# Second expert layer: results stored by token number, and down weights issued one position earlier

## The reference, cut to what matters

```python
def _route(hf, w_router, router_bias):
    scores = jax.nn.sigmoid((hf @ w_router).astype(jnp.float32))
    sel = scores + router_bias.astype(jnp.float32)
    grouped = sel.reshape(-1, N_GROUPS, EXPERTS_PER_GROUP)
    group_score = lax.top_k(grouped, TOP_K)[0].sum(-1)
    best = jnp.argmax(group_score, axis=-1)
    in_group = (jnp.arange(N_EXPERTS) // EXPERTS_PER_GROUP)[None, :] == best[:, None]
    _, idx = lax.top_k(jnp.where(in_group, sel, NEG_INF), TOP_K)
    w = jnp.take_along_axis(scores, idx, axis=-1)
    w = w / jnp.sum(w, axis=-1, keepdims=True)
    return jnp.sum(jax.nn.one_hot(idx, N_EXPERTS, dtype=jnp.float32) * w[..., None], axis=1)

def _moe(h, w_router, router_bias, w_gate, w_up, w_down):
    ...
    combine = _route(hf, w_router, router_bias).astype(h.dtype)
    y = jnp.zeros_like(hf)
    for e in range(N_EXPERTS):
        a = jax.nn.silu(hf @ w_gate[e]) * (hf @ w_up[e])
        y = y + combine[:, e:e + 1] * (a @ w_down[e])
    return y.reshape(shp)

# in the second layer, and then the end of the program:
x = x + g2 * _moe(_modulate(x, norm2[l], sh2, sc2), w_router, router_bias,
                  w_e_gate[l], w_e_up[l], w_e_down[l])
return _rmsnorm(x, final_norm)
```

## Time and profile before

| what | us |
|---|---|
| median of three runs | 1684.38 |
| the profiled execution | 1684.62 |
| its span | 1682.6 |
| outside the span | 2.0 |
| PE busy | 1587.2 (94%) |
| second layer's expert stage, from the first up_gate to the last landed result rows | 1395.9 to 1657.8 |

### The profile page before, as it was taken

One profiled execution on the slowest core, in us unless ns is written; L12 is line 12 of the kernel. 1 busy time (PEld: TensorE's weight loads), 2 busy tenths in 40 slices (PEclk: granted clock), 3 DMA queues, 4 the chain that ended last, 5 costly groups with the idle time before them and its releaser, 6 DMA issues. The chain is left out here.

```text
span 1682.6 us, 16523 instructions
## 1 busy us (share of the span) xinstructions
PE 1587.2 (94%) x6162; PEld 751.8 (45%) x6162; DVE 670.0 (40%) x1608; ACT 341.5 (20%) x782; POOL 123.6 (7%) x193
## 2 busy tenths in 40 slices
PE   5999999999999999899999979999999989998994
PEld 2444456544444445644444434445644445333331
DVE  2430068866677733511100145307867144111113
ACT  1210078820000021110100023007710021000001
POOL 1000000200000010200000020000200100110101
PEclk9999999999999999899999989999999999998998
DMA  9812141115545461699999996222178758999995
GB/s 345 273 50 100 50 168 66 39 51 150 201 151 200 150 225 48 244 349 366 386 391 393 366 355 202 100 100 76 39 227 324 276 193 292 370 388 392 389 360 210
DMA packets 176128, 380.83 MB, mean 226 GB/s; under 512 B 24430, under 2 KB 28670, under 8 KB 175912
## 3 DMA queue, kind: packets, MB, share of 16 engines
q1 hardware_dynamic: 160768, 327.17, 54.9%
q0 software_dynamic: 14272, 50.20, 7.8%
q10 hardware_dynamic: 1008, 2.38, 0.4%
HBM read 362.74 MB, written 26.80 MB: 232 GB/s over the span
## 5 line engine op out<-in xcount | busy, mean ns | idle before, releaser
L1881 PE MATMUL bank<-ring_sb,HT_sb 128*128 128x512 f32 x672 | 298.4, 599 | 3.1 <-ACT HT_sb L847 2.5
L1988 PE MATMUL bank<-ring_sb,HT_sb 128*128 128x512 f32 x544 | 240.6, 595 | 0.0
L1881 PEld LDWEIGHTS bank<-ring_sb,HT_sb 128*128 128x128 f32 x672 | 126.8, 193 | 151.8 <-issue 150.1
L1988 PEld LDWEIGHTS bank<-ring_sb,HT_sb 128*128 128x128 f32 x544 | 102.3, 190 | 135.7 <-issue 135.7
L1992 PE MATMUL bank<-ring_sb,QR_sb 128*128 128x512 f32 x288 | 129.5, 592 | 0.0
L2153 PE MATMUL bank<-ring_sb,HT_sb 128*64 128x512 f32 x480 | 106.5, 596 | 2.8 <-DMA ring_sb<-w_e_up 2.8
L2171 PE MATMUL bank<-ring_sb,QR_sb 128*128 128x512 f32 x208 | 97.8, 626 | 6.5 <-DMA ring_sb<-w_e_down 6.5
L973 ACT ACTIVATE WK_sb<-bank 128x512 f32<-128x512 f32 x36 | 21.5, 597 | 348.6 <-PE bank L1988 348.6
L2134 PE MATMUL bank<-ring_sb,HT_sb 128*128 128x512 f32 x192 | 85.4, 598 | 2.7 <-ACT HT_sb L1007 2.7
L2177 PE MATMUL bank<-ring_sb,QR_sb 128*64 128x512 f32 x304 | 73.8, 630 | 12.6 <-DMA ring_sb<-w_e_down 10.6
L1992 PEld LDWEIGHTS bank<-ring_sb,QR_sb 128*128 128x128 f32 x288 | 54.8, 190 | 68.8 <-issue 68.8
(11 more groups left out here) (336 smaller groups left out, 1708.7 us busy)
## 6 DMA issues: line engine op xcount, KB each, us to landing
ring_sb<-w_e_down SPq DMA_DIRECT2D x32, 2048.0 KB, 17.2
ring_sb<-w_mod SPq DMA_DIRECT2D x24, 2048.0 KB, 9.4
ring_sb<-w_in SPq DMA_DIRECT2D x22, 2048.0 KB, 15.0
ring_sb<-w_e_gate SPq DMA_DIRECT2D x16, 2048.0 KB, 14.8
ring_sb<-w_e_up SPq DMA_DIRECT2D x16, 2048.0 KB, 18.9
ring_sb<-w_e_gate SPq DMA_DIRECT2D x22, 1024.0 KB, 16.4
ring_sb<-w_e_up SPq DMA_DIRECT2D x22, 1024.0 KB, 14.6
ring_sb<-w_branch SPq DMA_DIRECT2D x8, 1024.0 KB, 9.9
```

Source lines behind the costliest of these rows:

```text
L1881: ins = mm(bank[j % 4][:, :], HT[:, k, P * t:P * t + P], WR[slot][:, k], start=(k == 0), stop=(k == KD - 1))
L1988: ins = mm(bank[i % 2][:, :], HT[:, k, P * t:P * t + P], WR[wg][:, k], start=(k == 0), stop=(k == KD - 1))
```

## The change

Two things change, both for the second layer alone.

- SP issues down weight q - 1 behind pair q (for q from 3 to 14), not q - 2; at q = 15 only down weight 14 stands ahead of pair 15.
- A result row is stored at the row of its token: at row `token` for the token's first expert and at `256 + token` for its second. POOL does this with an indirect DMA for each position, by the index `y_of`, and empty places get an index out of bounds and are skipped. A half position is stored in half rows, with 128 indices. Afterwards the four loads of the result rows are plain DMAs of 512 KB. Rows of tokens that sit in positions 14 and 15 are not written, so the whole table of 1280 rows is filled beforehand, as 20 copies of 64 rows of x, where 128 rows were filled before. The indices need 12 more small matmuls on PE and some small DVE operations.

```diff
@@ own_stores
-    return 0 if q >= NE - 2 else 1 if full_rows(l, q) else 2
+    return 0 if q >= NE - 2 else 1 if l or full_rows(l, q) else 2
@@ SP
-                    lag = 2 if l else 1
                     if q == NE - 1:
-                        for late in range(q - lag, q):
-                            load_expert(l, late, at[late], 2)
+                        load_expert(l, q - 1, at[q - 1], 2)
                     load_pair(l, q, at[q])
-                    if 2 * lag <= q < NE - 1:
-                        load_expert(l, q - lag, at[q - lag], 2)
+                    if 2 + l <= q < NE - 1:
+                        load_expert(l, q - 1, at[q - 1], 2)
@@ POOL, fill
-                dma(y_d[l][first_row(l, NE - 2):first_row(l, NE)], t_in["x"][0, 0:CAP]).then_inc(rows_set, 16)
+                    dma(y_d[l][first_row(l, NE - 2):first_row(l, NE)], t_in["x"][0, 0:CAP]).then_inc(rows_set, 16)
+                else:
+                    some = t_in["x"][:, 0:HALF].broadcast_to([first_row(l, NE) // HALF, HALF, D])
+                    dma(y_d[l][0:first_row(l, NE)].rearrange("(c p) d -> c p d", p=HALF), some).then_inc(rows_set, 16)
@@ POOL, stores
-                    if full_rows(l, q):
+                    if l:
+                        full = full_rows(l, q)
+                        table = y_d[l][0:2 * nq * P]
+                        eng.indirect_dma_start(table if full else table.rearrange("r (h n) -> (r h) n", h=2),
+                                               bass.IndirectOffsetOnAxis(ap=y_of[full][:, q:q + 1], axis=0),
+                                               yd[q % 2] if full else yd[q % 2][:, 0:CW], None,
+                                               bounds_check=2 * nq * P * (1 if full else 2) - 1, oob_is_err=False)\
+                            .then_inc(y_out[q % 2], 16)
+                    elif full_rows(l, q):
@@ POOL, result rows
-                    gather_outputs(y_d[l][0:first_row(l, NE)])
+                    if l == 0:
+                        gather_outputs(y_d[l][0:first_row(l, NE)])
+                    else:
+                        for t in range(nq):
+                            for k in range(2):
+                                dma(ygat[t][k], y_d[l][P * (nq * k + t):P * (nq * k + t + 1)]).then_inc(ygat_in[t], 16)
@@ DVE
+                    ts(y_of[0][:, :], bank[2][:, 2 * NE:3 * NE], 2.0, lower, ALU.mult, ALU.add)
+                    ts(y_of[1][:, :], bank[2][:, NE:2 * NE], float(MISSING), None, ALU.add)
                     ts(row_of[:, :], bank[2][:, 0:NE], float(MISSING), None, ALU.add).then_inc(slot_ready, 1)
@@ PE
+                    numbers(bank[2][:, 0:NE], P, token_at[:, 1])
+                    numbers(bank[2][:, NE:2 * NE], P, second_at)
+                    numbers(bank[2][0:HALF, 2 * NE:3 * NE], HALF, second_at)
+                    numbers(bank[2][HALF:P, 2 * NE:3 * NE], HALF, second_at).then_inc(pos_mm, 1)
```

More of the change, by code:

```diff
@@ L270, in build @@
         row_of = sb("row_of", [P, NE], I32)
+        y_of = [sb(f"y_of{i}", [P, NE], I32) for i in range(2)]
         sp_idx = sb("sp_idx", [P, 1], I32)
@@ L313, in build @@
         token_at = MB[:, 608:608 + NLAT * NE].bitcast(F16).rearrange("p (k t q) -> p k t q", k=2, t=NLAT)
-        token_no = MB[:, 784:784 + NLAT]
+        token_no = MB[:, 784:784 + 2 * NLAT].rearrange("p (k t) -> p k t", k=2)
+        second_at = MB[:, 640:640 + NLAT * NE // 2].bitcast(F16).rearrange("p (t q) -> p t q", t=NLAT)
+        y_row = MB[:, 788:788 + 2 * NLAT].rearrange("p (k t) -> p k t", k=2)
+        lower = MB[:, 792:793]
         gout_half = MB[:, D:D + CW]
@@ L1545, in _ @@
                     link(tt(r_two[:, :, 0:nq], r_row.unsqueeze(1).unsqueeze(1).broadcast_to(pick), r_o12[:, :, 0:nq], ALU.mult))
-                    ts(token_no, tabh[:, H_TOK:H_TOK + nq], -float(MISSING), None, ALU.add)
+                    for k in range(2):
+                        ts(token_no[:, k], tabh[:, H_TOK:H_TOK + nq], float(nq * P * k - MISSING), None, ALU.add)
+                        ts(y_row[:, k], tabh[:, H_TOK:H_TOK + nq], float(nq * P * k), None, ALU.add)
+                    ts(lower, tabh[:, H_TOK:H_TOK + 1], float(HALF), 2.0 * MISSING, ALU.is_ge, ALU.add)
                     link(eng.tensor_reduce(where, r_two[:, :, 0:nq], AX, ALU.add))
@@ L1550, in _ @@
                     for t in range(nq):
-                        ts(token_at[:, :, t], at_place[:, :, t], token_no[:, t:t + 1], None, ALU.mult)
+                        ts(token_at[:, :, t], at_place[:, :, t], token_no[:, 0, t:t + 1], None, ALU.mult)
+                        ts(second_at[:, t], at_place[:, 1, t], token_no[:, 1, t:t + 1], None, ALU.mult)
                     wide = [P, 2, nq, P]
@@ L1577, in _ @@
                 link(tt(share, weight, held_last, ALU.mult))
-                tt(slot_g[:, :, 0:nq], slots, at, ALU.subtract)
+                if l == 0:
+                    tt(slot_g[:, :, 0:nq], slots, at, ALU.subtract)
+                else:
+                    link(tt(r_two[:, :, 0:nq, 0], slots, y_row, ALU.subtract))
+                    link(stt(r_two[:, :, 0:nq, 1], slots, float(first_row(l, NE)), r_two[:, :, 0:nq, 0], ALU.is_ge, ALU.mult))
+                    tt(slot_g[:, :, 0:nq], r_two[:, :, 0:nq, 1], y_row, ALU.add)
                 tt(weight, weight, share, ALU.subtract)
@@ L2194, in _, with numbers @@
                     eng.wait_ge(pick_ready, 5)
-                    for i in range(2 * nq):
-                        ins = mm(bank[2][:, 0:NE], in_place[:, i // nq, i % nq], token_at[:, i // nq, i % nq],
-                                 start=(i == 0), stop=(i == 2 * nq - 1))
-                    ins.then_inc(pos_mm, 1)
+                    def numbers(dst, places, of_second):
+                        for i in range(2 * nq):
+                            k, t = divmod(i, nq)
+                            ins = mm(dst, in_place[:, k, t, 0:places], of_second[:, t] if k else token_at[:, k, t],
+                                     start=(i == 0), stop=(i == 2 * nq - 1))
+                        return ins
+                    numbers(bank[2][:, 0:NE], P, token_at[:, 1])
+                    numbers(bank[2][:, NE:2 * NE], P, second_at)
+                    numbers(bank[2][0:HALF, 2 * NE:3 * NE], HALF, second_at)
+                    numbers(bank[2][HALF:P, 2 * NE:3 * NE], HALF, second_at).then_inc(pos_mm, 1)
                 transpose_rows(1)
```

2 lines of the change are left out of this document (1 added, 1 removed).

## The result

The changed kernel takes 1693.92 us (median of 9 runs, 1689.71 to 1696.02) beside 1685.76 for the kernel before (9 runs, 1683.24 to 1690.47). The ratio is 1.0043, with a 95% interval from 1.0032 to 1.0054: 7.2 us slower (the two medians alone would give 1.0048). I had predicted 1685.6 us and no difference that can be measured. In all that follows a ratio is turned into us with 1685.4, the median of the 17 runs of before that stand beside the first experiments.

The account below looks back on a forecast made before the run. The prediction took DMA bandwidth (391 GB/s), not PE, to bound the second expert stage. Terms +10.7 - 1.6 - 3.3 - 6.7 + 0.9 + 1.2 = +1.2 us on 1684.38 gave 1685.6 us; range 1682 to 1688, widened to 1677 and 1691.

Parts of the forecast that it names:

- The step that failed: Second layer's expert stage: DMA sets the end, so each change in bytes counts as time at 391 GB/s.
- Down weight 2 ahead of pair 4: Early in the stage, pair 4 now waits behind down weight 2, which waits for down(0): cost 10.7 us, bounds 0 to 10.7.
- The debt: Pair 4's 4.19 million bytes still owed at 1438 us, 10.7 us of DMA, never repaid as DMA is full to the end.
- The rival that had it shrink: Pair 4's delay does not reach the end: sum -4.2 us if halved, -9.5 if none; 1676 us, chance 0.27.
- The thin stretch: From 1439 to 1455 us DMA moved 351 GB/s with little queued; a fuller queue gains 1.6 us.
- The pause before pair 15: From 1625 to 1633 us DMA moved 229 GB/s; the new order fills this and gains 3.3 us, bounds 0 to 3.3.
- Stores: Second layer's result stores fall from 4.72 to at most 2.10 MB, as skipped places move no data: 6.7 us saved.
- skipped places save nothing: Rival: from 1438 to 1642 us scatters pay for empty places too; sum +7.9 us, 1692.3 us, chance 0.14.
- Indices: 12 more small matmuls behind up_gate(0) and two index operations ahead of `row_of`, on PE's path to down(0): cost 0.9 us.
- The end: Result loads and final norm, issued earlier, go in ahead of the last weight, which lands last: cost 1.2 us, bounds -0.2 to 1.2.
- The fill: Table fill of 5.24 MB from 1141.19 us, done before DVE reads bias tiles at 1188.71: costs 0.
- The clock: Rival: a wait over 3 us at up_gate(15) slows PE for down(15), up to 3 us, 1688.7; chance 0.12 with a late fill.

Follow-up runs that it names:

- reverse: The kernel before with the new order of down weights up to position 8 and the old one from 9 on: ratio 1.0061 to the kernel before, +10.3 us.
- hybrid: The kernel before with the old order of down weights up to position 7 and the new one from 8 on: ratio 0.9995 to the kernel before, -0.8 us.
- order_only: The kernel before with only the new order of down weights, stores, gathers and fill as before: ratio 1.0067 to the kernel before, +11.3 us.
- dense: The changed kernel, but empty places are written to table rows that nobody reads, not skipped: ratio 1.0066 to the kernel before, +11.1 us.
- guard: The changed kernel, but POOL starts result loads and final norm only once the last down weight has landed: ratio 1.0034 to the kernel before, +5.7 us.
- stride8: The changed kernel with an expert's n-th token on row 8(n mod 8) + n div 8 of its 64-row half: ratio 1.0058 to the kernel before, +9.8 us.
- spread: The changed kernel with an expert's n-th token on row 4(n mod 16) + n div 16 of its 64-row half: ratio 1.0042 to the kernel before, +7.1 us.

## Why the prediction was wrong, by its own steps

**The step that failed** is the one all terms share: bytes divided by the mean rate of the 16 engines (391 GB/s), where the end follows the engine that is furthest behind. By halves, the order had +7.0 in its terms and measured +11.3, and the stores with their indices had -5.8 and measured -4.0, so the larger part of the miss lies in the order. By terms:

- *Down weight 2 ahead of pair 4, +10.7*: right. SP's rows in after show the step, down weight 2 and pair 4 right behind it:

```profile
1439.16 0.37 SPq L550 DMA_DIRECT2D ring_sb<-w_e_down  x1
1440.32 0.38 SPq L565 DMA_DIRECT2D ring_sb<-w_e_gate  x1
```

  The debt alone, reverse against before, is 9.5 at pair 15 where debt and thin stretch gave 9.1, and it was never repaid. The rival that had it shrink is refuted.
- *The thin stretch, -1.6*: less came of it. 2.6 us later in after, to be held against the 351 GB/s of the earlier trace rows, the row below has 368, which over 16 us is 0.7 us.

```profile
1441.60:1457.60 16.00, 16.00 (x66) 6.35 (x64) 2.40 (x4) 1.19 (x2) 2.56 (x4) 1.00 1.03 368
```

- *The pause before pair 15, -3.3*: up to pair 15 the size is about right, 3.3 at the last part in hybrid and 2.3 between reverse and order_only. But the pause was also what levelled the engines, and 1.8 of it (hybrid against before) or 2.3 (order_only against reverse) were lost again between pair 15 and the last weight. Without it the parts spread over 6.0 to 7.3 us in every kernel, for 1.6 to 2.3 where there is one.
- *Stores, -6.7*: the bytes are right (POOL's queue 6.19 MB from 1437 to 1646 before, 3.55 MB from 1441 to 1646 after; predicted 2.62 less, found 2.64). The mean engine gains 6.4 (order_only to after at pair 15), the last one 4.5, because the skipped rows do not lie on all engines alike. The rival "skipped places save nothing" is refuted (dense). That its figure, +7.9, is near the measured 7.2 is luck.
- *Indices, +0.9*: nothing found. The 16 small matmuls took 0.58 us in a place where PE's path had room:

```profile
1411.89 0.58 PE L2227 MATMUL bank<-MB_sb,QR_sb 128*128 128x16 f16 x16
```

  down(0) started 33.9 us after the first `up_gate`, and 33.5 before; 0.4 at most.
- *The end, +1.2*: undersized. From pair 15's last part to the last weight's last part it is 5.9 us in before, 9.0 in after, 5.0 in guard. So the result loads cost 4.0 us in after, and 3.1 more than in before (about 0.9 there, if guard's 5.0 holds for level engines too, which no run shows). I had POOL issue them earlier, and it did so by only 0.5 us; and I had let them share with 16 even engines, where those that were behind carried their part of the loads in turn with the weight.
- *The fill, 0*: right. The additions start at 1170.39, 27 us after the fill was issued, far ahead of 1188. The rule of the Trainium skill ("DMA: Bandwidth & Descriptors", Why a DMA increments its semaphore by 16 and not by 1) for 20 copies (10 engines, an estimate of 20 us) fits this better than the 5 engines of the earlier trace rows: from 1146 to 1160 the queue moved 3.28 MB at a share of 54.7%, that is over 5 engines.

```profile
q0 software_dynamic: 104, 3.28, 54.7%
```

- *The clock*, which I had as a rival with a price of up to 3 us: it came at down(15), behind its own wait of 3.14 us, and cost 1.7; the waits of up_gate(15), which I had named, were 2.04 and 1.71. (1685.6 + 3 is 1688.6, not 1688.7.) I had also misapplied what the Trainium skill ("TensorE: Matmul & The Clock Gate", HAM oscillation — how this bites in real kernels) says of loops that compute less than they wait. PE computed about 12 us of each 16.8, so it does not say that the half positions would run cold, and most of their down products took 3.65 us. The long stretch had more but shorter waits and a higher clock (0.99 for 0.93), which gained nothing, as DMA set the pace there.

The sum in after, from the table: the last part of pair 15 +2.8 (predicted 0.0; 1.5 of it by the order, 1.3 by the stores), the end +3.1 (1.2), together +5.9 for the last landing. Of that 0.5 is slack that before had: its last weight landed at 1656.04, 0.58 us ahead of down(15), where in after it is 0.04. (The prediction took the start at 1656.62 for the landing.) Then the clock +1.7. 5.9 - 0.5 + 1.7 = 7.1, which is the 7.0 of the rows, and 7.2 was measured. Of the 6.0 us that the prediction lacked, 2.8 are the engines that were behind at pair 15, 1.9 the result loads on those engines, 1.7 the clock, less 0.5.

What stays open: which engines are late, how an indirect DMA deals its rows out to them, and why stride8's transfers were slower.

## What to carry to other kernels

A transfer that is cut over 16 engines has landed when the slowest has. In a stretch where DMA is always busy, add the saved bytes up for the mean engine, then ask how far the last one is behind, and look at the fading of the share after the stretch for it. A short pause in the queue is not all waste, since it levels the engines. A small load that comes in late beside the last large one costs more when the engines are not level. When two edits come together, time each alone: here one was worth 4 us and the other cost 11.

## What I had not expected of the hardware

- With even loads (before) the 16 parts of one transfer drift apart from 2.1 to 5.8 us within 170 us, some 0.4 us for each position. In the twelve kernels without a pause near the end the spread at pair 15 is 6.0 to 7.3 us, and never more; perhaps because SP can't issue further ahead, which no run tried.
- Rows skipped by an indirect DMA free only some engines. Six, four or two of sixteen were late, as the rows lay.
- Result loads of 2.6 MB beside the last weight cost it 4.0 us when the engines were not level (after against guard), and by an estimate from the same numbers 0.9 us in before, where they were.
- down(15) took 5.35 us after an idle time of 3.14 or 3.12 us (3.65 at full clock); after 1.87 us (spread) or 0.35 us it took 3.65. But the length of the last wait alone doesn't decide it. The earlier trace rows suggest a limit between 2.32 and 2.93 us; in after a wait of 2.76 us left the clock alone, and 2.04 us did not:

```profile
1537.64 3.65 PE L2206 MATMUL bank<-ring_sb,QR_sb 128*64 128x512 f32 x16 [2.76 <-DMA ring_sb<-w_e_down]
...
1555.07 5.35 PE L2206 MATMUL bank<-ring_sb,QR_sb 128*64 128x512 f32 x16 [2.04 <-DMA ring_sb<-w_e_down]
```
